# Half slots of an attention stage: all projection steps first, then one block of plain fp32 matmuls and transposes

## The chip, the cores and the metric

The kernel runs on one core of one Trainium2 chip. The metric is the device time of one execution in microseconds (us). The kernel before took 2443.29 us, the median of three runs between 2438.51 and 2446.40 us.

## The reference

The reference is a decoder trunk of two layers over x of 1 x 1024 x 1024 in float32. All of it is causal.

```python
for layer in range(2):
    h = rmsnorm(x, norm_mix[layer])
    x = x + (even_mixer if layer == 0 else swa_mixer)(h, ...)
    h = rmsnorm(x, norm_mlp[layer])
    x = x + square(relu(h @ w_up[layer])) @ w_down[layer]      # hidden width 4096
```

- `even_mixer` projects h by one matrix. Four retention heads (query and key of 64, value and gate of 128) get a rotation, chunks of 128 tokens with a decay matrix and a state that is carried from chunk to chunk, a group norm and a silu gate. Eight heads of width 64 get RMSNorm and rotation of query and key, and attention over a mixture of three dilated windows, (128, 1), (512, 4) and (2048, 16). The two outputs are concatenated and multiplied by `w_out`.
- `swa_mixer` projects to 16 query heads and 4 key and value heads of width 64, with a bias, RMSNorm and rotation; each query sees the last 128 keys; a learned sink adds to the softmax denominator; then an output projection.

## The kernel before

The 1024 tokens are T = 8 tiles of 128 rows. x stays on chip in `X`. The normed input of a stage lies transposed in `hT_hi` and `hT_lo`, and weights lie in `W_hi` and `W_lo`: each fp32 operand is split in two fp32r parts, and one product is three matmuls (`three`, L457 to L461: hi by hi, hi by lo, lo by hi). Scores, transposes, probabilities by values and the whole of retention are plain fp32 matmuls or transposes through `ident`, with no split.

**Two attention stages.** The first (`dr_slots`) holds the dilated heads, two at a time, and the retention heads, one at a time, in NG = 4 groups. A group is 16 slots of projections (8 token tiles of the dilated columns, then 8 of the retention columns), and its other work follows a slot or more behind, so `live` gives for a slot one or two pairs (g, t), t being the slot's number in group g. The second (`s_slots`) holds the sliding window heads, 32 slots of projections and 4 more. Each slot does one projection of 128 tokens by 384 columns: `gemm_steps` is a generator of 8 steps, each step being the three matmuls of one 128-row part of the input (L478 to L492). A slot has two halves, j = 0 and j = 1, with four steps each. Between the steps TensorE does:

- `scores` of attention unit n = 2t + j - 4 (L511, into `sc`), `trans` of unit n - 1 (its probabilities transposed, L543, into `tp`) and `values` of unit n - 2 (L551, into `o_ps`). A unit is one tile of queries with one head (dilated: a + 1 blocks of keys for query tile a, so 1 to 8) or two heads (sliding window: 2 blocks of keys at most each).
- `heads_T` (L564) in the second half: the queries and keys of the tile projected in the slot before are transposed into `qt`.
- retention of chunk r = t - 9: `ret_T` (L570, transposes, at the start of the second half), `ret_scores` (L579, end of the second half), `ret_values` of chunk r - 1 (L587, first half).
- `first_T`, `tile_T`, `norm_T`, `mixed_T`: transposes of whole token tiles where a stage joins its neighbour. `mixed_T` (L494) does so by halves in the slots from O1_T = 30 of the second stage, through `qt`.

**Who waits for whom.** There is no planner; the order is written out by hand, each engine has its own copy of the loop, and semaphores join them. The diff touches TensorE's loop only. For one unit: VectorE reads the scores and makes the masked maximum (`maxima`, L1418 or L1423), ScalarE the exponentials (`probs`, L891 or L898), TensorE `trans`, ScalarE copies `tp` (`probs_T`, L883), TensorE `values`, VectorE scales into `X` (`outputs`, L1440 or L1449). `sc`, `tp`, `o_ps` and `qt` are single buffers. So `scores` waits for the maximum of the unit before (`sm_ready`), and `values` for the scaled output of the unit before (`o_evac`). In VectorE's queue `outputs` of unit n - 3 stands first in a half slot, then `sums`, `maxima` of unit n, `prep` (norm and rotation of the tile's queries and keys, L1389 to L1406, behind GpSimd's L1792, and read by `heads_T`), `ret_rope` (L1331 to L1350, read by `ret_T` from L1340 on) and `ret_out` (L1366 to L1373, behind `ret_values`; it ends in the semaphore `r_x`). `ret_state` (L1354, L1361), behind `ret_scores`, stands in the second half. ScalarE ends a first half with the hi parts of new weights (L827) and a second half with the copies of `qt` (`heads_T_copy`, L905, L907), and opens the slot with the copy of the projection out of PSUM (`evac_G`, L855; in the second stage VectorE does it, L1494) and `head_squares` (L871). GpSimd makes the lo parts of the weights (L1735). The first `head_squares` of a later group waits for the last `ret_out` of the group before, since both use `sq`.

The MLP after each attention stage, and the output projections, are the rest of the kernel; the change does not touch them.

Of the kernel before, what the change touches and what calls it, by code (L numbers as in the profile page):

```python
# [29 lines left out]
def hybrid_trunk(nc, x_in, positions, norm_mix, norm_mlp, w_up, w_down, w_in, w_out0, gn_gain, dq_gain, dk_gain,  # L30
# [7 lines left out]
    S, D = x_in.shape[1], x_in.shape[2]  # L38
    T = S // P
# [49 lines left out]
    with ctx:  # L89
# [166 lines left out]
        def unit(n):  # L256

            return n // (2 * T), n % (2 * T) // 2, n % 2
# [195 lines left out]
        def _(pe):  # L454
# [87 lines left out]
            def trans(kind, n, u0):  # L542
                g, a, j = unit(n)  # L543
                pe.wait_ge(p_ready, u0 + n + 1)
                if u0 + n >= 1:
                    pe.wait_ge(pt_ready, u0 + n)
                for c, to, _, _ in blocks(kind, a):
                    last = nc.tensor.transpose(tp[:, to:to + P], Pm[:, j, c:c + P], ident[:, :])  # L548
                last.then_inc(tp_done, 1)

            def values(kind, n, u0):  # L551
                g, a, j = unit(n)
                pe.wait_ge(pt_ready, u0 + n + 1)
                pe.wait_ge(v_ready, (u0 // 2 if kind == "D" else A_S + (u0 - U_S) // 2) + n // 2 + 1)
                if u0 + n >= 1:
                    pe.wait_ge(o_evac, u0 + n)
                bl = blocks(kind, a)
                v0 = HD * j if kind == "D" else 0
                for m, (_, to, c, e) in enumerate(bl):
                    last = mm(o_ps[:, e * HD:(e + 1) * HD], pT[:, j, to:to + P], V[:, c, v0:v0 + HD],  # L560
                              start=(m == 0 or bl[m - 1][3] != e), stop=(m == len(bl) - 1 or bl[m + 1][3] != e))
                last.then_inc(pv_done, 1)
# [7 lines left out]
            def ret_T(r, n):  # L570

                pe.wait_ge(r_qk, n + 1)
                alone(pe)
                q, k, qx = rQK[:, r % 2, 0:HD], rQK[:, r % 2, HD:2 * HD], QK[:, r % 2, 4 * HD:5 * HD]
                for m, src in enumerate((q, k, qx)):
                    last = nc.tensor.transpose(qt[0:HD, m * P:(m + 1) * P], src, ident[:, :])
                last.then_inc(r_qt, 1)
# [20 lines left out]
            def first_T(s, q):  # L598

                for i in range(T):  # L600
                    if FIRST_T[i] == (s, q):
                        if i in FIRST_DVE:
                            pe.wait_ge(first_dve, FIRST_DVE.index(i) + 1)
                        else:
                            pe.wait_ge(first_pool, FIRST_POOL.index(i) + 1)
                        tile_T(first_xn[i % 6], i, 0, 0)
# [3 lines left out]
            def dr_slots():  # L610

                for s in range(DR_SLOTS):
                    now = live(s)
                    g, t = now[-1]
                    if s < NG * 2 * T:
                        steps = gemm_steps(N_DR + s, t // T, t % T, W, P_DR + 8 * g + 4 * (t // T), 0)
                    else:
                        steps = gemm_steps(N_O0 + s - NG * 2 * T, 0, s - NG * 2 * T, W, P_O0, T)
                    for j in range(2):
                        for g, t in now:  # L620
                            r = t - T - 1
                            if j == 1 and 0 <= r < T:
                                ret_T(r, g * T + r)
                        if s < 2 and j == 0:
                            first_T(s, 0)
                        next(steps)
                        next(steps)
                        if s < 2:
                            first_T(s, 2 * j + 1)
                        for g, t in now:  # L630
                            n, r = 2 * t + j - 4, t - T - 1
                            if 0 <= n < 2 * T:
                                scores("D", n, g * 2 * T)
                            if 0 <= n - 1 < 2 * T:
                                trans("D", n - 1, g * 2 * T)
                            if j == 0 and 0 <= r - 1 < T:
                                ret_values(r - 1, g * T + r - 1)
                        next(steps)
                        for g, t in now:
                            n = 2 * t + j - 4  # L640
                            if 0 <= n - 2 < 2 * T:
                                values("D", n - 2, g * 2 * T)
                        next(steps)
                        if s < 2:
                            first_T(s, 2 * j + 2)
                        for g, t in now:
                            r = t - T - 1
                            if j == 1 and 0 <= r < T:
                                ret_scores(r, g * T + r, g)
                            if j == 1 and 0 <= t - 1 < T:  # L650
                                heads_T("D", t - 1, g * T)
                        if j == 1 and s >= O0_T:

                            pe.wait_ge(r_x, (NG - 1) * T + s - O0_T + 1)
                            tile_T(X[:, s - O0_T, :], s - O0_T, T, 2)

            def s_slots():

                units = NG * 2 * T
                for t in range(S_SLOTS):  # L660
                    c = t // T
                    if t < NG * T:
                        steps = gemm_steps(N_S + t, c % 2, t % T, W, P_S + 4 * c, 3 * T)
                    else:
                        steps = gemm_steps(N_O1 + t - NG * T, 0, t - NG * T, W, P_O1, 4 * T)
                    for j in range(2):
                        n = 2 * t + j - 4
                        next(steps)
                        next(steps)
                        if t == 0:  # L670

                            norm_T(2, T - 2 + j, 3 * T, 1)
                        if 0 <= n < units:
                            scores("S", n, U_S)
                        if t >= O1_T:
                            mixed_T(t - O1_T, 4 * T, j)
                        if 0 <= n - 1 < units:
                            trans("S", n - 1, U_S)
                        next(steps)
                        if 0 <= n - 2 < units:  # L680
                            values("S", n - 2, U_S)
                        next(steps)
                        if j == 1 and 0 <= t - 1 < units // 2:
                            if t >= O1_T:
                                pe.wait_ge(ht_ready, 4 * T + t - O1_T + 1)
                            heads_T("S", t - 1, A_S)
# [1327 lines left out]
```

## Time and profile before

| | |
|---|---|
| runs | 2446.40, 2438.51, 2443.29 us |
| profiled execution | 2441.46 us, of which the span from the first to the last instruction is 2439.7 us |
| PE busy | 2365.9 us (97%), 12184 matmul records |
| PE weight loads busy | 1991.1 us (82%) |
| VectorE, ScalarE, GpSimd busy | 1464.0 (60%), 834.6 (34%), 1099.8 us (45%) |
| chain that ended last, by engine | PE 82%, DVE 10%, POOL 3%, issue 2%, ACT 2%, DMA 1% |
| granted TensorE clock, mean | 0.994 |

A busy share says how long records of an engine were open. For PE the records overlap: the next matmul starts while the last is still draining, so the distance from start to start tells what a matmul costs, and the length of a record does not. A plain fp32 matmul shows as two records. The bracket at the end of a timeline row gives how long that engine was idle just before and which instruction ended the idleness.

### The profile page before, as it was taken

The numbers are of one execution on the slowest core, as the hardware profiler recorded it, in microseconds if no ns is written. First come the engines' busy times: TensorE is split into PE (matmuls) and PEld (weight loads), VectorE is DVE, ScalarE is ACT, GpSimd is POOL, SyncE is SP. The second block draws the span as 40 slices with busy tenths as digits, with TensorE's granted clock in tenths as the row PEclk, the third lists the DMA queues.
The fourth block names the chain that finished last, engine by engine and source line by source line (L and its number), as shares of the span: only waits on it lengthen the run. The fifth ranks groups of instructions, "written<-read, shape, count | busy, mean of one in ns | idle before, by whom it ended". The sixth has DMA issues, their size and how long they took to land.

```text
span 2439.7 us, 34453 instructions
## 1 busy us (share of the span) xinstructions
PE 2365.9 (97%) x12184; PEld 1991.1 (82%) x12184; DVE 1464.0 (60%) x2846; ACT 834.6 (34%) x1717; POOL 1099.8 (45%) x994
## 2 busy tenths in 40 slices
PE   6999999999999999999999899999999999999999
PEld 5777878777987888888888788888977888888887
DVE  7464645546148757675774566663356676667573
ACT  5424333342132322332232455553232232223230
POOL 5123131311227646664673733431245574557461
PEclk9999999999999999999999999999999999999999
DMA  4001010102221021102101300012021102110201
GB/s 136 14 27 27 27 27 14 33 7 87 65 70 52 18 69 60 60 17 69 60 26 57 114 26 24 27 35 91 27 69 61 61 17 69 60 60 17 83 29 78
DMA packets 140981, 120.35 MB, mean 49 GB/s; under 512 B 26048, under 2 KB 126912, under 8 KB 140864
## 3 DMA queue, kind: packets, MB, share of 16 engines
q1 hardware_dynamic: 133488, 103.70, 13.7%
q10 hardware_dynamic: 7376, 15.12, 1.8%
q8 instruction: 70, 1.15, 0.2%
q14 instruction: 47, 0.39, 0.1%
HBM read 110.41 MB, written 8.39 MB: 49 GB/s over the span
## 4 chain that ended last, share of the span: by engine, by line
PE 82%; DVE 10%; POOL 3%; issue 2%; ACT 2%; DMA 1%; SPq 0%; DVEq 0%; ACTq 0%; POOLq 0%
PE gp L459 12%; PE gp L461 12%; PE gp L460 12%; PE sc L459 6%; PE sc L461 6%; PE sc L460 6%; PE o_ps L560 4%; PE sc L526 3%; PE tp L461 2%; PE tp L460 2%; PE tp L459 2%; PE tp L548 2%; PE sc L531 1%; PE qt L461 1%; PE qt L459 1%
## 5 line engine op out<-in xcount | busy, mean ns | idle before, releaser
L459 PE MATMUL gp<-W_hi,hT_hi 128*128 128x384 f32 (+1 forms) x1152 | 423.1, 367 | 6.0 <-DVE hT_lo L1307 6.0
L461 PE MATMUL gp<-W_hi,hT_lo 128*128 128x384 f32 (+1 forms) x1152 | 384.7, 334 | 0.0
L460 PE MATMUL gp<-W_lo,hT_hi 128*128 128x384 f32 (+1 forms) x1152 | 384.0, 333 | 0.0
L1860 POOL TENSOR_TENSOR W_lo<-af,W_hi 128x512 fp32r<-128x512 f32 x168 | 237.5, 1413 | 283.2 <-ACT W_hi L1041 283.2
L1840 POOL TENSOR_TENSOR W_lo<-raw,W_hi 128x1024 fp32r<-128x1024 f32 x72 | 187.2, 2604 | 237.9 <-ACT W_hi L983 225.1
L1554 DVE TENSOR_TENSOR af<-af 128x512 f32<-128x512 f32 x112 | 81.0, 725 | 297.8 <-ACT af L1024 297.7
L1860 POOL TENSOR_TENSOR W_lo<-rb,W_hi 128x512 fp32r<-128x512 f32 x168 | 243.6, 1450 | 0.0
L459 PEld LDWEIGHTS gp<-W_hi,hT_hi 128*128 128x128 f32 x1152 | 221.3, 192 | 15.0 <-issue 6.8
L460 PEld LDWEIGHTS gp<-W_lo,hT_hi 128*128 128x128 f32 x1152 | 221.8, 192 | 0.0
L461 PEld LDWEIGHTS gp<-W_hi,hT_lo 128*128 128x128 f32 x1152 | 219.8, 191 | 0.0
L459 PE MATMUL sc<-hT_hi,W_hi 128*128 128x512 f32 x512 | 200.1, 391 | 5.3 <-DVE hT_lo L1307 5.3
L461 PE MATMUL sc<-hT_hi,W_lo 128*128 128x512 f32 x512 | 199.9, 390 | 0.0
L460 PE MATMUL sc<-hT_lo,W_hi 128*128 128x512 f32 x512 | 199.7, 390 | 0.0
L459 PE MATMUL gp<-hT_hi,W_hi 128*128 128x512 f32 x512 | 199.5, 390 | 0.2 <-POOL W_lo L1840 0.2
L461 PE MATMUL gp<-hT_hi,W_lo 128*128 128x512 f32 x512 | 199.2, 389 | 0.0
L460 PE MATMUL gp<-hT_lo,W_hi 128*128 128x512 f32 x512 | 199.2, 389 | 0.0
L1735 POOL TENSOR_TENSOR W_lo<-raw,W_hi 128x768 fp32r<-128x768 f32 (+1 forms) x70 | 124.4, 1779 | 136.1 <-ACT W_hi L827 135.8
L1041 ACT ACTIVATE W_hi<-af 128x512 fp32r<-128x512 f32 x168 | 105.8, 630 | 165.2 <-PE sc L461 89.4
L883 ACT ACTIVATE pT<-tp 128x512 f32<-128x512 f32 (+7 forms) x128 | 78.3, 612 | 244.9 <-PE tp L548 244.9
L1024 ACT ACTIVATE af<-gp 128x512 f32<-128x512 f32 x56 | 33.4, 601 | 340.3 <-PE gp L461 340.3
L560 PEld LDWEIGHTS o_ps<-V,pT 128*128 128x128 f32 x1056 | 134.8, 191 | 16.1 <-ACT pT L883 8.0
L560 PE MATMUL o_ps<-V,pT 128*128 128x64 f32 x1056 | 133.3, 270 | 10.9 <-DVE X L1440 8.8
(292 smaller groups left out, 5262.7 us busy)
## 6 DMA issues: line engine op xcount, KB each, us to landing
raw<-in_mlp_w_up SPq DMA_DIRECT2D x64, 512.0 KB, 4.2
rb<-in_mlp_w_down SPq DMA_DIRECT2D x56, 512.0 KB, 5.0
raw<-in_hyb_w_in SPq DMA_DIRECT2D x74, 128.0 KB, 2.4
X<-in_x SPq DMA_DIRECT2D x8, 512.0 KB, 7.4
X<-in_x ACTq DMA_DIRECT2D x8, 512.0 KB, 3.4
raw<-in_mlp_w_down SPq DMA_DIRECT2D x8, 512.0 KB, 3.3
raw<-in_swa_w_qkv SPq DMA_DIRECT2D x16, 256.0 KB, 3.2
x_spill<-X ACTq DMA_DIRECT2D x8, 512.0 KB, 2.7
```

The source lines that it names most:

```text
L459: mm(o, a[0], b[0], start=first, stop=False)
L460: mm(o, a[0], b[1], start=False, stop=False)
L461: return mm(o, a[1], b[0], start=False, stop=last)
L526: last = mm(sc[:, c:e], qT[r, a % 2, 0:P], kT[r, c:e], start=True, stop=True)
L548: last = nc.tensor.transpose(tp[:, to:to + P], Pm[:, j, c:c + P], ident[:, :])
L560: last = mm(o_ps[:, e * HD:(e + 1) * HD], pT[:, j, to:to + P], V[:, c, v0:v0 + HD], start=(m == 0 or bl[m - 1][3] != e), stop=(m == len(bl ...
L883: A(pT[:, n % 2, 0:w], tp[:, 0:w], ACT.Copy).then_inc(pt_ready, 1)
L1041: A(WF_hi[:, op_at(side, 2 * p + k)], x(k), ACT.Copy).then_inc(op_hi, 1)
L1554: E.tensor_tensor(x, x, x, ALU.mult).then_inc(a_sq, 1)
L1735: E.tensor_tensor(W_lo[:, slot, c], raw[:, p % 2, 0:n], W_hi[:, slot, c].bitcast(f32), ALU.subtract).then_inc(w_ready, 1)
L1840: E.tensor_tensor(WF_lo[:, at], raw[:, j % 2, :], WF_hi[:, at].bitcast(f32), ALU.subtract).then_inc(w_ready, 1)
L1860: E.tensor_tensor(WF_lo[:, c], x(k), WF_hi[:, c].bitcast(f32), ALU.subtract).then_inc(op_ready, 1)
```

## The change

In `dr_slots` of TensorE a half slot did, before: `ret_T` (second half), two steps, `scores`, `trans` and `ret_values`, one step, `values`, one step, then `ret_scores` and `heads_T`. Now it does four steps, then `scores`, `trans`, `values`, `ret_values`, then `ret_T` at the end of the first half or `ret_scores` and `heads_T` at the end of the second. The transposes of the first slots (`first_T`) keep their place. In `s_slots` the third and fourth step move ahead of `scores`, `mixed_T`, `trans` and `values`. No instruction is added or removed, and no other engine's order changes.

```diff
                     for j in range(2):
-                        for g, t in now:
-                            r = t - T - 1
-                            if j == 1 and 0 <= r < T:
-                                ret_T(r, g * T + r)
                         if s < 2 and j == 0:
                             first_T(s, 0)
                         next(steps)
                         next(steps)
                         if s < 2:
                             first_T(s, 2 * j + 1)
+                        next(steps)
+                        next(steps)
+                        if s < 2:
+                            first_T(s, 2 * j + 2)
                         for g, t in now:
                             n, r = 2 * t + j - 4, t - T - 1
                             if 0 <= n < 2 * T:
                                 scores("D", n, g * 2 * T)
                             if 0 <= n - 1 < 2 * T:
                                 trans("D", n - 1, g * 2 * T)
+                            if 0 <= n - 2 < 2 * T:
+                                values("D", n - 2, g * 2 * T)
                             if j == 0 and 0 <= r - 1 < T:
                                 ret_values(r - 1, g * T + r - 1)
-                        next(steps)
-                        for g, t in now:
-                            n = 2 * t + j - 4
-                            if 0 <= n - 2 < 2 * T:
-                                values("D", n - 2, g * 2 * T)
-                        next(steps)
-                        if s < 2:
-                            first_T(s, 2 * j + 2)
                         for g, t in now:
                             r = t - T - 1
+                            if j == 0 and 0 <= r < T:
+                                ret_T(r, g * T + r)
                             if j == 1 and 0 <= r < T:
                                 ret_scores(r, g * T + r, g)
```

```diff
                             norm_T(2, T - 2 + j, 3 * T, 1)
+                        next(steps)
+                        next(steps)
                         if 0 <= n < units:
                             scores("S", n, U_S)
                         if t >= O1_T:
                             mixed_T(t - O1_T, 4 * T, j)
                         if 0 <= n - 1 < units:
                             trans("S", n - 1, U_S)
-                        next(steps)
                         if 0 <= n - 2 < units:
                             values("S", n - 2, U_S)
-                        next(steps)
```

## Rows read from the trace of the kernel before

**Rows 1.** Windows: length, then busy us (count) by engine, clock, DMA share, GB/s.

```profile
41.00:600.00 559.00, 533.89 (x3014) 437.38 (x3015) 306.77 (x968) 208.83 (x466) 149.71 (x219) 0.99 0.10 29
1384.00:1690.00 306.00, 294.84 (x1955) 254.24 (x1956) 197.39 (x847) 157.40 (x508) 104.66 (x141) 0.99 0.12 34
```

**Rows 2.** Groups of instructions, projection matmuls: busy us, mean ns, idle before.

```profile
L459 PE MATMUL gp<-W_hi,hT_hi 128*128 128x384 f32 (+1 forms) x1152 | 423.1, 367 | 6.0 <-DVE hT_lo L1307 6.0
L461 PE MATMUL gp<-W_hi,hT_lo 128*128 128x384 f32 (+1 forms) x1152 | 384.7, 334 | 0.0
```

**Rows 3.** Timeline of PE, sliding window, one second half: start us, duration us.

```profile
1520.04 0.70 PE L531 MATMUL sc<-kT,qT 64*128 64x256 f32 x4
1520.67 0.66 PE L548 MATMUL tp<-ident,Pm 128*128 128x128 f32 x4
...
1521.52 0.34 PE L461 MATMUL gp<-W_hi,hT_lo 128*128 128x384 f32 x1
1521.69 1.00 PE L560 MATMUL o_ps<-V,pT 128*128 128x64 f32 x8
...
1522.76 0.34 PE L460 MATMUL gp<-W_lo,hT_hi 128*128 128x384 f32 x1
1522.94 0.33 PE L461 MATMUL gp<-W_hi,hT_lo 128*128 128x384 f32 x1
1523.11 0.49 PE L567 MATMUL qt<-ident,QK 128*128 128x128 f32 x3
...
1523.61 0.34 PE L460 MATMUL gp<-W_lo,hT_hi 128*128 128x384 f32 x1
```

**Rows 4.** Waits of PE in 41 to 600 us: us, times, longest.

```profile
PE qt L567 <- DVE QK L1401: 10.3, 4, 3.1
PE o_ps L560 <- DVE X L1440: 8.8, 12, 1.1
PE sc L592 <- DVE rsT L1354: 1.8, 6, 0.3
```

**Rows 5.** Waits of PE in 1380 to 1700 us.

```profile
PE qt L567 <- DVE hT_lo L1293: 5.4, 3, 1.9
...
PE sc L531 <- ACT kT L907: 0.8, 2, 0.6
```

**Rows 6.** Timeline where the second group of the first stage begins.

```profile
172.80 0.38 PE L592 MATMUL sc<-G,rsT 128*128 128x128 f32 x2
...
173.64 0.30 DVE L1366 BATCH_NORM_STATS2 st<-sc 128x6 f32<-128x128 f32 x1 [1.35 <-PE sc L595]
...
180.07 0.69 PE L567 MATMUL qt<-ident,QK 128*128 128x128 f32 x2 [3.15 <-DVE QK L1401]
```

**Rows 7.** Timeline, group 1, slot t = 10 (first chunk of retention meets the last unit).

```profile
263.54 0.39 PE L592 MATMUL sc<-G,rsT 128*128 128x128 f32 x2
...
265.30 0.29 DVE L1366 BATCH_NORM_STATS2 st<-sc 128x6 f32<-128x128 f32 x1
...
269.49 0.29 PE L560 MATMUL o_ps<-V,pT 128*128 128x64 f32 x1 [0.79 <-DVE X L1440]
```

**Rows 8.** Timeline, group 1, slot t = 9: scores, the rotation's end, `ret_T`.

```profile
248.38 0.69 PE L526 MATMUL sc<-kT,qT 64*128 64x512 f32 x1
...
252.77 0.25 DVE L1340 TENSOR_SCALAR QK<-rQK,st 128x64 f32<-128x64 f32 x1
...
253.71 0.38 PE L576 MATMUL qt<-ident,rQK 128*64 128x128 f32 x2
```

**Rows 9.** Timeline, group 1, slots t = 2 and 3: copies of `qt`, `values` of unit 1.

```profile
188.82 0.28 ACT L905 ACTIVATE qT<-qt 128x128 f32<-128x128 f32 x1 [0.57 <-PE qt L567]
...
195.53 0.41 PE L560 MATMUL o_ps<-V,pT 128*128 128x64 f32 x2 [0.94 <-DVE X L1440]
```

**Rows 10.** Timeline of DVE in the half slot of rows 3.

```profile
1520.05 0.29 DVE L1449 TENSOR_TENSOR X<-o_ps,st 128x128 f32<-128x128 f32 x1
```

**Rows 11.** Windows, the stretch around the third group's start.

```profile
319.00:329.00 10.00, 8.34 (x38) 7.52 (x39) 4.68 (x15) 3.98 (x13) 4.10 (x5) 0.83 0.08 21
```

## The prediction

> **What bounds the kernel now.** I read the page first: PE is busy for 97% of the span and makes up 82% of the chain that ended last, so TensorE's own work sets the time, and a wait of PE is paid in full. Then the windows of the two stages that the change touches: PE is busy 534 of 559 us in the first and 295 of 306 us in the second [rows 1]. About 25 and 11 us are idle; that is all that any better order could win from waits. The list of waits says which instruction ends the idleness; most of it is VectorE, at five or six kinds of places [rows 4, 5]. Last I read the timeline around each kind of place, to see from which event the chain that PE waits for starts. The change removes nothing, so two questions are left: does a boundary between fp32r steps and plain fp32 work cost PE anything, and how many microseconds of projection lie, before and after, between the start of a chain and the instruction that waits for its end.
>
> **Boundaries.** The number of separate plain blocks falls: `values` joins `trans` (64 units in each stage, 128 blocks), `heads_T` joins `values` (64), `ret_T` joins `ret_values` (32), so about 224 blocks vanish. What is one worth? The page tempts: L459, the first matmul of each step, shows 367 ns where L461 shows 334 [rows 2], because an L459 behind plain work is drawn longer. But starts decide. Between two projection matmuls lie 0.174 us (1522.76 to 1522.94 rounds it to 0.18). From L461 at 1521.52 over eight records of `values` to L460 at 1522.76 are 1.24 us; take off two projection intervals of 0.174 and 0.89 is left, 0.112 per record. The block of three transposes, 1522.94 to 1523.61, leaves 0.67 - 0.35 = 0.32, or 0.108 each [rows 3]. A fixed price per block would make the block of eight cheaper per record than the block of three; it is not. The boundary costs 0 to 0.02 us. A joint from a transpose straight to a values record is nowhere in the trace. From below: a record hidden behind its neighbour saves 0.08 us, times 128 is 10 us. From above: it costs one record of the kind that the scores show, 0.63 us for four [rows 3], so 0.16, times 128 is 20 us. I take 0, since the records on both sides run at the same 0.11, and keep both ends.
>
> The Trainium skill speaks against long plain blocks: "TensorE: Matmul & The Clock Gate", Part 4: PE-mode transpose, says that transposes do not count as work for the clock. No window of rows 1 shows a mean clock under 0.99; what it would do here is the fourth case below.
>
> **Waits, place by place.** One step is three matmuls at 0.174, so 0.52 us. I count steps from the event that starts a chain to the PE instruction at its end.
>
> 1. *Start of groups 1, 2 and 3.* `ret_values` of the last chunk (172.80) starts the chain over `ret_out`, `head_squares`, `sums`, GpSimd and `prep` to `heads_T` at 180.07, 7.27 us, in which PE stood idle 3.15 us. VectorE had waited 1.35 us for `ret_values` [rows 6], so the chain really starts there. `ret_values` moves from behind two steps to behind four, `heads_T` stays at the end of the slot. The chain starts 1.04 us later: 3 x 1.04 = +3.1 us. Queued behind the waiting `heads_T` are only the next slot's steps, which nobody else needs early.
> 2. *Slot t = 10, four groups.* `values` of unit 15 waits 0.79 us for `outputs` of unit 14, which stands in VectorE's queue behind `ret_out` of chunk 0, and that behind `ret_values` (263.54). VectorE was late on its own and began `ret_out` at 265.30, 1.76 us after `ret_values` began [rows 7]. Now `ret_values` comes two steps (1.04) later, and behind `values` of unit 14, 16 records of 0.112, 1.8 us, which it used to precede: 2.8 us later, with the chain starting 0.4 us after its beginning, so 2.8 - 1.76 + 0.4 = 1.5 us later than now. PE gets to `values` of unit 15 one step later than before in the slot, 0.5. So +1.0 per group, +4.0 us.
> 3. *Slot t = 9, four groups.* `ret_T` of chunk 0 needs `ret_rope`, which VectorE does after the maximum of unit 14. From scores 14 (248.38) the rotation's end (253.02) takes 4.64 us, and `ret_T` starts 5.33 us after the scores [rows 8]. Two steps of the 5.33 move ahead of the scores: 4.29 us are left, 0.35 short, 0.45 with the semaphore. +1.8 us.
> 4. *Slots 30 to 32 of the second stage.* `heads_T` waits for the lo half of `mixed_T` (L1293), 5.4 us in three waits [rows 5]. The chain starts with the scores of the first half slot (maximum, exponentials, copy, lo half, `prep`, `outputs`, and the same in the second half), and two steps move out from between: 3 x 1.04 = +3.1 us.
> 5. *Slots t = 3 and 4 of each group.* Eight of the twelve waits for L1440 are `values` of units 1 and 3, 0.94 us at 195.53. The chain starts at `heads_T` of the slot before, whose copies ScalarE waited 0.57 us for [rows 9]. `heads_T` now comes two steps sooner after the scores, so ScalarE copies as soon as it has its exponentials, about 0.55 us sooner; `values` loses one step, 0.52. Unit 1: 0. Unit 3 comes a slot later in full, gains 0.4 and had 0.24 to wait (0.70 in the first group): -1.0 us in all, between -1.4 and 0.
> 6. *Retention slots.* `ret_values` waits 1.8 us in all for L1354 [rows 4]. It gets two steps more of cover. `ret_T` keeps its distance and becomes the next limit, some 0.4 us further on in each group: -1.5 us, at best -1.8, at worst 0.
> 7. *Second stage, scores behind the copy of `kT`*: 0.8 us [rows 5], two steps more cover, -0.8 us. Elsewhere in this stage the scaled output is done at 1520.34 and `values` comes at 1521.69, 1.35 us in hand; `prep` stands ahead of that output in the queue, so `heads_T` at 1523.11 has over 3 [rows 3, 10]. They lose 0.5 and 1.0: nothing, unless ScalarE, which now meets `heads_T` before it has done the exponentials, runs late; it has about 0.3 us.
> 8. *Clock.* Around one group start the granted clock is 0.83 over 10 us [rows 11]: after the idle stretch the lower level, 1.2 of 2.4 GHz, held for a third of the window, worth up to 1.7 us. Of the six waits in points 1 and 4 four were followed by such a stretch. With a microsecond more each, I count the other one or two in as well: +1.5 us, 0 to +3.
>
> SP's queue and the weight loads follow the steps, whose order against each other and against the slots does not change; DMA keeps 10 to 12% busy [rows 1]. So no transfer moves by more than 2 us, under a slot of lead.
>
> **Sum.** 3.1 + 4.0 + 1.8 + 3.1 - 1.0 - 1.5 - 0.8 + 1.5 = +10.2 us. Against the profiled execution, 2441.5 (span 2439.7 and 1.8 around it), that is 2451.7; this execution lies 1.8 us under the median of the three runs, so the median should come to 2453.5. I say 2453. The positive terms could each fail by a half (-6) or be doubled by their neighbours (+6).
>
> **Rivals.**
> - *The boundary does cost.* A plain block ends with a first projection matmul drawn 0.09 us longer (0.42 against 0.33), and 33 ns times 1152 of L459 are 38 us in the stages with 416 such blocks [rows 2]. If that were time on PE, 224 blocks fewer would win 20 us, less the 10 lost in waits: 2433, faster. It decides if the count of blocks times 0.09 is real; the start-to-start sums speak against it, unless a joined block streams faster than 0.108 a record. 12%.
> - *The waits do not grow.* Every chain starts from an event that moves with the waiting instruction, as in point 5; points 2 to 4 then vanish and point 1 alone stays, with points 6 and 7 against it: +1 to +4, 2446. For it: four places of point 5 work so. Against: VectorE's own waits say where a chain begins in points 1 and 3. 25%.
> - *Joints are dear.* 0.16 us at each of 128 joints adds 20 us: 2474. For it: scores followed by transposes take longer than their records. Against: there the operand's height changes from 64 to 128 rows, here it stays 128. 5%.
> - *Clock.* The longest joined blocks, units 10 to 15 in four groups, are over 3.5 us without a projection matmul. If such a block drops the clock to the lower level as the idle stretches do, at 1.2 to 1.7 us each, 24 blocks add 29 to 41 us: about 2488. The blocks before were up to 2.8 us and no clock fell after one. 4%. The page of the Trainium skill named above would have it so.
>
> **Numbers.** The forecast has 54%, its own range 2445 to 2464. About 0.3%, 7.3 us, is what a measurement of this kernel tells from no change. Faster takes nearly all of the first rival: 0.11. Within 0.3% takes the second and the low third of the forecast's range: 0.30. Slower has the rest: 0.59. The range that leaves out the boundary rival's and the clock's centre and little more is 2440 to 2469.
>
> **What would show it.** PE's records keep their counts; L459's mean falls from 367 towards 350 ns while the distance of starts per step stays 0.52 us. In the waits, L567 behind L1401 grows from 10.3 to 13.4 us, behind L1293 from 5.4 to 8.5, L560 behind L1440 from 8.8 to about 12, with unit 15 at 1.8; L592 and L531 vanish; L576 waits 0.4 us in slot t = 9. If PE's idle time in the two windows grows by 10 us and the time does not, the boundary is worth something. If idle time does not grow, the chains began elsewhere than I say. A transpose followed by a values record at more than 0.12 us shows the dear joint; a clock under 0.99 over the first stage shows the fourth rival.

## The result, and the profile after

The changed kernel takes 2453.15 us, median of seven runs (2450.02 to 2458.45), against 2443.78 us (2438.51 to 2446.40) for the kernel before in the same sessions: ratio 1.0039, 95% interval 1.0029 to 1.0048. That is 0.4% slower and clear of the noise. The forecast was 2453. The profiled execution has a span of 2451.8 us against 2439.7, 12.1 us more, with a mean granted clock of 0.986 against 0.994.

Lines of the changed file are four lower than before (L1436 is `outputs`, L1397 and L1402 end `prep`, L1336 ends the rotation, L1289 is the lo half). The windows of the two stages and the projection groups, to be laid beside [rows 1, 2]:

```profile
41.00:600.00 559.00, 527.49 (x2943) 441.24 (x2944) 285.76 (x944) 202.77 (x463) 148.83 (x216) 0.96 0.10 28
1384.00:1690.00 306.00, 293.92 (x1941) 254.99 (x1939) 190.33 (x840) 155.09 (x508) 112.80 (x152) 0.98 0.11 32
```

```profile
L459 PE MATMUL gp<-W_hi,hT_hi 128*128 128x384 f32 (+1 forms) x1152 | 407.4, 354 | 5.6 <-POOL W_lo L1731 5.0
L461 PE MATMUL gp<-W_hi,hT_lo 128*128 128x384 f32 (+1 forms) x1152 | 388.0, 337 | 0.0
```

In the same 559 us PE gets through 2943 records where it did 3014, and the clock is 0.96 where it was 0.99. The waits of PE in the first stage (first fence) and in the second, beside [rows 4, 5]:

```profile
PE qt L567 <- DVE QK L1397: 13.8, 4, 4.2
PE o_ps L560 <- DVE X L1436: 9.5, 7, 1.8
PE qt L576 <- DVE QK L1336: 8.0, 12, 1.0
```

```profile
PE qt L567 <- DVE hT_lo L1289: 7.1, 3, 2.5
...
PE sc L531 <- ACT kT L903: 1.4, 4, 0.9
PE o_ps L560 <- DVE X L1445: 1.2, 3, 0.4
```

The waits that were forecast are there: `heads_T` at the group starts has gone from 3.1 to 4.2 us, the longest wait of `values` from 1.1 to 1.8 us, L592 no longer waits. The timeline of slot t = 10 in group 1, VectorE and PE, beside [rows 7]:

```profile
265.83 1.90 PE L560 MATMUL o_ps<-V,pT 128*128 128x64 f32 x16
...
267.56 0.44 PE L592 MATMUL sc<-G,rsT 128*128 128x128 f32 x2
267.84 0.38 PE L576 MATMUL qt<-ident,rQK 128*64 128x128 f32 x2
268.04 0.30 DVE L1362 BATCH_NORM_STATS2 st<-sc 128x6 f32<-128x128 f32 x1 [1.41 <-PE sc L592]
...
271.77 0.28 DVE L1436 TENSOR_SCALAR X<-o_ps,st 128x64 f32<-128x64 f32 x1
272.20 0.52 PE L560 MATMUL o_ps<-V,pT 128*128 128x64 f32 x3 [1.79 <-DVE X L1436]
```

`ret_values` of chunk 0 (L592) now stands behind the 16 records of `values` 14. VectorE, which used to come to it late, waits 1.41 us for it, and 4.2 us later PE waits 1.79 us for what VectorE makes at the end of that chain.

Behind that wait something stands that was not in the forecast. Windows over the wait and what follows it (length, then busy us and count by engine, granted clock, DMA share, GB/s):

```profile
270.00:272.00 2.00, 0.41 (x3) 0.09 (x1) 1.93 (x4) 1.47 (x3) 1.52 (x1) 1.00 0.00 0
272.00:273.00 1.00, 0.80 (x6) 0.83 (x6) 0.06 (x1) 0.15 (x1) 0.00 (x0) 0.81 0.24 68
273.00:279.00 6.00, 6.00 (x23) 5.33 (x23) 2.05 (x11) 0.00 (x0) 0.00 (x0) 0.50 0.19 54
```

The granted clock falls within half a microsecond of the end of the wait and stays down for 6.8 us. The first records that it slows are the plain ones of `values` 15, whose starts go from 0.11 to 0.21 us apart. Timeline of PE 5 us further on:

```profile
277.23 0.52 PE L460 MATMUL gp<-W_lo,hT_hi 128*128 128x384 f32 x1
277.55 0.52 PE L461 MATMUL gp<-W_hi,hT_lo 128*128 128x384 f32 x1
277.87 0.52 PE L459 MATMUL gp<-W_hi,hT_hi 128*128 128x384 f32 x1
```

Projection matmuls start 0.32 us apart, where 0.174 is the rule, so the clock is at the lower of its two levels, 1.2 of 2.4 GHz. No such stretch followed `values` 15 in any group of the kernel before.

To weigh these things I cut the first stage at `heads_T` of slot t = 1 of each group. The first three groups, from 38.3 us on, take 421.9 us before and 430.7 after. Of them PE is idle 19.4 and 25.5 us, and projection matmuls with starts over 0.3 us apart lose 3.7 and 6.1 us against 0.174. The rest, 398.8 and 399.0, looks unchanged, but it holds the plain records, which the lower clock slows too. Groups with no slowed projection matmul at all occur in several traces: 132.4 and 132.6 us each without idle time in the order of before (kernel `s_apart` below), 130.6 and 130.7 in the order of after (`ret_first`, where only two neighbours inside a block are swapped, and `d_only`). So at full clock a group is 1.85 us shorter after, and the low clock costs three groups about 5 us before (3.7 and 1.3 in plain records) and 13 after (6.1 and 7.0). The granted clock itself says much the same: in these groups PE worked at the lower level for 12.6 us before and 30.8 after, and at 0.146 us lost in every 0.32 that is 6 and 14 us.

### The profile page after: what moved, and what is told of

Read it like the earlier page. It is cut to its first block, busy times and chain, and to the rows that moved or that the text cites. A ratio compares the mean times of both kernels' runs of the same rounds, so it can differ in the third digit from the quotient of the medians.

```text
span 2451.8 us, 34453 instructions
## 1 busy us (share of the span) xinstructions
PE 2372.2 (97%) x12184; PEld 2009.4 (82%) x12184; DVE 1442.0 (59%) x2846; ACT 827.3 (34%) x1717; POOL 1102.0 (45%) x994
## 4 chain that ended last, share of the span: by engine, by line
PE 86%; DVE 7%; POOL 2%; issue 2%; ACT 2%; DMA 1%; SPq 0%; DVEq 0%; ACTq 0%; POOLq 0%
PE gp L459 13%; PE gp L461 13%; PE gp L460 13%; PE sc L459 6%; PE sc L460 6%; PE sc L461 6%; PE o_ps L560 4%; PE sc L526 3%; PE tp L548 3%; PE tp L460 2%; PE tp L459 2%; PE tp L461 2%; PE sc L531 2%; PE qt L459 1%; PE o_ps L459 1%
## 5 line engine op out<-in xcount | busy, mean ns | idle before, releaser
L459 PE MATMUL gp<-W_hi,hT_hi 128*128 128x384 f32 (+1 forms) x1152 | 407.4, 354 | 5.6 <-POOL W_lo L1731 5.0
L461 PE MATMUL gp<-W_hi,hT_lo 128*128 128x384 f32 (+1 forms) x1152 | 388.0, 337 | 0.0
L460 PE MATMUL gp<-W_lo,hT_hi 128*128 128x384 f32 (+1 forms) x1152 | 387.4, 336 | 0.0
L459 PEld LDWEIGHTS gp<-W_hi,hT_hi 128*128 128x128 f32 x1152 | 223.2, 194 | 12.7 <-issue 7.8
L460 PEld LDWEIGHTS gp<-W_lo,hT_hi 128*128 128x128 f32 x1152 | 223.6, 194 | 0.0
L461 PEld LDWEIGHTS gp<-W_hi,hT_lo 128*128 128x128 f32 x1152 | 222.6, 193 | 0.0
L459 PE MATMUL sc<-hT_hi,W_hi 128*128 128x512 f32 x512 | 200.1, 391 | 5.3 <-DVE hT_lo L1303 5.3
L460 PE MATMUL sc<-hT_lo,W_hi 128*128 128x512 f32 x512 | 199.9, 390 | 0.0
L461 PE MATMUL sc<-hT_hi,W_lo 128*128 128x512 f32 x512 | 199.8, 390 | 0.0
L459 PE MATMUL gp<-hT_hi,W_hi 128*128 128x512 f32 x512 | 199.4, 389 | 0.0
L461 PE MATMUL gp<-hT_hi,W_lo 128*128 128x512 f32 x512 | 199.2, 389 | 0.0
L460 PE MATMUL gp<-hT_lo,W_hi 128*128 128x512 f32 x512 | 199.2, 389 | 0.0
```

The lines of the kernel that those rows point to most:

```text
L459: mm(o, a[0], b[0], start=first, stop=False)
L460: mm(o, a[0], b[1], start=False, stop=False)
L461: return mm(o, a[1], b[0], start=False, stop=last)
```

## Experiments

The theory at the start, A: the time moves by how many projection steps lie between the start of a chain and the PE instruction at its end; boundaries are free. B: each boundary between fp32r and plain work costs 0.09 us. C: the long joined blocks themselves lower the clock.

**The two stages apart.** `s_only` has the new `s_slots` and the old `dr_slots`, `d_only` the other way round; the lines are those of the change.

```diff
 # s_only: s_slots as changed, dr_slots as before
 # d_only: dr_slots as changed, s_slots as before
```

> The changed order in the sliding window stage alone. Theory A (what moves the time is how many projection steps lie between the start of a chain and the PE instruction that waits for it; a block boundary costs nothing): the trace of the full change had in this stage 0.3 us more idle time, 1.9 us more of slowed projection matmuls and 8 slots shorter by 0.5 us when idle time is taken out, so +0.5 to +2 us on 2443.8, no difference that can be told. Rival B (a boundary between fp32r and plain fp32 costs 0.09 us): 96 boundaries fewer in 32 slots, -8.6 us plus the same 2: about 2437. Rival C (long plain blocks by themselves lower the clock): blocks of 2.1 us with every half slot, so +5 us and more with a clock under 1.00 in the steady slots.

> The changed order in the dilated and retention stage alone. Theory A: +10 to +12 us, nearly all of the full change (2454 to 2456), with the same waits as there: heads_T 4.19 us at three group starts, values of unit 15 1.8 us at four places, ret_T 0.38 us at four. Rival B: 128 boundaries fewer here, -11 us beside waits of +6.5 and slowed matmuls of +5.7: about 2445. Rival C: as A in the sum, but the slowed matmuls follow the longest blocks (units 10 to 15), not the idle stretches.

Measured beside 2441.67 us for the kernel before: `s_only` 2446.31 us, ratio 1.0015 (1.0005 to 1.0024), and `d_only` 2454.09 us, 1.0041 (1.0027 to 1.0054). Nearly all of the loss is the first stage's. The interval of `s_only` leaves out 1, but its trace does not put that time into the second stage: the stage takes 294.5 us before and 295.7 in `s_only`, within the 0.5 to 2 us expected, and the rest of the 5.9 us between the spans stands ahead of it, where the code is the same, PE's idle time grew by 0.4 us and the clock was lower. In the second stage eight steady slots are 68.0 us without idle time instead of 68.5, with the clock at 1.00 all through, so C is not seen there and B is far too large; slots 30 to 32 give the gain back. In `d_only` the waits are those of the full change. The slowed matmuls stood behind the idle stretches, not behind the longest blocks, in three groups of four; in the first group there were none.

**`ret_values` alone goes back.** All attention blocks stay joined.

```diff
                             first_T(s, 2 * j + 1)
+                        for g, t in now:
+                            r = t - T - 1
+                            if j == 0 and 0 <= r - 1 < T:
+                                ret_values(r - 1, g * T + r - 1)
                         next(steps)
...
-                            if j == 0 and 0 <= r - 1 < T:
-                                ret_values(r - 1, g * T + r - 1)
```

> The full change, but ret_values goes back behind the second step of the first half slot, as before the change. Every attention block stays joined. Theory A: the wait at the three group starts falls from 4.19 to 3.15 us (-3.1), that of values 15 from 1.8 to about 0.3 (-6), the slowed matmuls behind values 15 go (-5), the joint of ret_values and ret_T is lost (+1.6) and ret_values may wait 0.3 us again in a few slots: 2440 to 2443. Rival C (the joined blocks lower the clock): slowed matmuls stay, 2445 to 2448. If the loss had to do with scores, values and heads_T standing together: no change, 2453.

2434.58 us, ratio to before 0.9960 (0.9945 to 0.9975), 18.6 us under the changed kernel. The same change with this one instruction group left in its place is faster than the kernel before. (That is against the changed kernel's own session; each beside the kernel before in its session, it is 19.3 us.) Waits of PE in its first stage, and the window:

```profile
PE qt L567 <- DVE QK L1399: 12.3, 6, 3.2
PE qt L576 <- DVE QK L1338: 5.1, 9, 0.8
PE o_ps L560 <- DVE X L1438: 2.7, 5, 1.0
```

```profile
41.00:620.00 579.00, 552.99 (x3162) 460.93 (x3162) 302.17 (x981) 211.36 (x473) 158.38 (x226) 0.99 0.12 34
```

Against the changed kernel the three groups are 17.9 us shorter: 7.5 of idle time, 13 of clock, and 2.6 back for `ret_values` standing alone again. I had expected 10 to 13; the waits came as said, and the clock is what I had too small.

**Which part of the placement.** `ret_first` keeps the four steps and puts `ret_values` ahead of `values`; `ret_last` moves only the last chunk of a group back behind two steps. Both edits are against the changed kernel.

```diff
 # ret_first
+                            if j == 0 and 0 <= r - 1 < T:
+                                ret_values(r - 1, g * T + r - 1)
                             if 0 <= n - 2 < 2 * T:
                                 values("D", n - 2, g * 2 * T)
-                            if j == 0 and 0 <= r - 1 < T:
-                                ret_values(r - 1, g * T + r - 1)
 # ret_last
+                        for g, t in now:
+                            if j == 0 and t == 2 * T + 1:
+                                ret_values(T - 1, g * T + T - 1)
                         next(steps)
...
-                            if j == 0 and 0 <= r - 1 < T:
+                            if j == 0 and 0 <= r - 1 < T - 1:
```

> The full change, but ret_values stands ahead of values in the block; it still comes after four steps. Theory A: VectorE begins ret_out of chunk 0 by its own lateness again, so the wait at values 15 falls from 1.8 to about 0.3 us in four places (-6), and with it the slowed matmuls behind that wait; the group starts keep 4.19 us. Of the 18.6 us between the full change and ret_values behind two steps this placement should win 10 to 12: about 2442. If the two steps alone matter and not the 1.8 us of values ahead: 2450 or more.

> The full change, but ret_values of the last chunk of each group alone (slot t = 17) goes back behind the second step. Theory A: the three waits at the group starts fall from 4.19 to 3.15 us (-3.1) and some of the slowed matmuls behind them go (0 to -4); the waits at values 15 stay 1.8 us. 2446 to 2450. With ret_first it should add up to the 18.6 us of both. If the clock falls for the long plain blocks, it changes nothing in the slowed matmuls.

`ret_first` 2442.61 us, ratio 0.9990 (0.9981 to 1.0000), `ret_last` 2449.02 us, 1.0021 (1.0011 to 1.0031), beside 2445.41. From 2453.15 they win 10.5 and 4.1 us, both within what was expected. Together 14.6 of 18.6, or 16.4 of 19.3 when each is taken by its ratio to the kernel before in its session; those sessions differ by 2 to 4 us in the kernel before, so the sum is not tested closer. The profile of `ret_last` is of its fastest run, 2440.63 us. Waits of `ret_first` (first fence) and of `ret_last`, first stage:

```profile
PE qt L567 <- DVE QK L1397: 13.8, 4, 4.2
PE qt L576 <- DVE QK L1336: 10.0, 15, 1.0
PE o_ps L560 <- DVE X L1436: 3.6, 6, 0.9
```

```profile
PE qt L567 <- DVE QK L1400: 10.7, 4, 3.2
PE o_ps L560 <- DVE X L1439: 9.5, 7, 1.8
```

Each touches one kind of wait and leaves the other.

**The one move alone.** The order of before, and only `ret_values` goes behind the fourth step. No attention block is joined.

```diff
-                            if j == 0 and 0 <= r - 1 < T:
-                                ret_values(r - 1, g * T + r - 1)
...
                         for g, t in now:
                             r = t - T - 1
+                            if j == 0 and 0 <= r - 1 < T:
+                                ret_values(r - 1, g * T + r - 1)
                             if j == 1 and 0 <= r < T:
                                 ret_scores(r, g * T + r, g)
```

> The order of before, with ret_values alone moved to behind the fourth step, where it joins ret_T. No attention block is joined. Theory A, as it now stands (waits, the clock after them, and 0.1 us for each ret_values that joins ret_T): the three waits at group starts grow to 4.2 us (+3.1), that of values 15 from 0.8 to 2.3 us (+6), the clock falls behind it in most groups (+4 to +8), 28 joints win 3: +10 to +14 us, 2454 to 2458 on 2443.8, so this one move is enough for the whole loss. Rival D (the loss needs the joined blocks too, since they lower the clock): the waits as said, but no slowed matmuls behind values 15: +5 to +6.

2465.99 us, ratio 1.0085 (1.0071 to 1.0099) beside 2445.66: +20.3 us, more than the full change and well over the 10 to 14 that I expected. The waits are as computed, the clock is not. Its waits and its window:

```profile
PE o_ps L560 <- DVE X L1440: 14.4, 12, 2.3
PE qt L567 <- DVE QK L1401: 12.8, 4, 4.2
```

```profile
41.00:620.00 579.00, 542.57 (x2999) 450.45 (x2999) 307.17 (x964) 210.17 (x469) 150.29 (x218) 0.96 0.10 28
```

This settles C. With no joined attention block, but 2.3 us of waiting at `values` 15, the low clock follows in three groups of four; in `ret_first`, with the same long block and 0.4 us of waiting (0.65 in the last group), in one. Over all twelve traces, four groups each: behind a wait of 1.8 us or more at that place, 12 of 16; behind 0.3 to 1.1 us, 1 of 32. It is the idle stretch, with or without the joined blocks.

**Boundaries doubled.** In the second stage `scores` moves ahead by a step, so that each part stands alone.

```diff
                         next(steps)
+                        if t < O1_T and 0 <= n < units:
+                            scores("S", n, U_S)
                         next(steps)
...
-                        if 0 <= n < units:
+                        if t >= O1_T and 0 <= n < units:
                             scores("S", n, U_S)
```

> The order of before; in the second stage up to slot 29 scores moves ahead by one step, so scores, transposes, values and heads_T each stand alone: two boundaries more per slot, some 60 in all. Theory A (a boundary costs 0 to 0.02 us): 0 to +1 for them, and the three waits of 0.70 us for the output fall to 0.2: 2441 to 2444, no difference that can be told; 8 slots of the steady part take 68.5 us without idle time, as before. Rival B (0.09 us each): +5.4, and 8 slots take 70 us without idle time.

2452.41 us, ratio 1.0038 (1.0026 to 1.0051) beside 2445.41. A is wrong here and B is nearer: eight steady slots take 69.8 us without idle time instead of 68.5, 1.3 us for 16 more boundaries, 0.08 each (B said 0.09). The rest is waiting: `scores` has a step less of cover behind the copy of `kT` and now waits 0.12 us in every first half. Timeline of PE in one half slot:

```profile
1505.15 0.34 PE L461 MATMUL gp<-W_hi,hT_lo 128*128 128x384 f32 x1
1505.42 0.70 PE L531 MATMUL sc<-kT,qT 64*128 64x256 f32 x4
1506.05 0.44 PE L459 MATMUL gp<-W_hi,hT_hi 128*128 128x384 f32 x1
1506.33 0.34 PE L460 MATMUL gp<-W_lo,hT_hi 128*128 128x384 f32 x1
1506.50 0.34 PE L461 MATMUL gp<-W_hi,hT_lo 128*128 128x384 f32 x1
1506.68 0.60 PE L548 MATMUL tp<-ident,Pm 128*128 128x128 f32 x4
1507.03 0.42 PE L459 MATMUL gp<-W_hi,hT_hi 128*128 128x384 f32 x1
1507.29 0.34 PE L460 MATMUL gp<-W_lo,hT_hi 128*128 128x384 f32 x1
1507.47 0.34 PE L461 MATMUL gp<-W_hi,hT_lo 128*128 128x384 f32 x1
1507.64 1.00 PE L560 MATMUL o_ps<-V,pT 128*128 128x64 f32 x8
...
1508.71 0.34 PE L460 MATMUL gp<-W_lo,hT_hi 128*128 128x384 f32 x1
```

The scores alone cost 1.18 - 0.35 = 0.83 us from L461 to L460, the values still 1.24 - 0.35 = 0.89 as in [rows 3]. The transposes alone cost 0.79 - 0.35 = 0.44 us, 0.11 each, which leaves nothing for a boundary. In this half slot the two come to 1.27 us where together they were 1.22. What the split adds stands with the scores: the boundary that costs is the one behind a 64-row operand.

**`values` behind the fourth step.** The order of before, with one step more of cover for `values`, in both stages. The diff shows the first; the second has the same move.

```diff
-                        for g, t in now:
-                            n = 2 * t + j - 4
-                            if 0 <= n - 2 < 2 * T:
-                                values("D", n - 2, g * 2 * T)
                         next(steps)
+                        for g, t in now:
+                            n = 2 * t + j - 4
+                            if 0 <= n - 2 < 2 * T:
+                                values("D", n - 2, g * 2 * T)
```

> The order of before, with one move in both stages: values goes from behind the third step to behind the fourth, so it joins heads_T, and everything else stays. Theory A: each wait of values falls by one step of 0.52 us: unit 1 of four groups 0.94 to 0.42, unit 3 to nothing (-1.4 in all), unit 15 0.8 to 0.3 (-2), and three of 0.7 to 0.2 in the second stage (-1.5): -5.5 to -7.5 us, about 2437. Rival B: 64 boundaries fewer besides, another -6: 2431. If what waits for values (the outputs, and behind them the maximum) then comes late, the gain is lost again: 2443.

2432.53 us beside 2441.67, ratio 0.9958 (0.9945 to 0.9971), 9.1 us. Waits of `values` fall from 10.9 to 4.0 us in all, 6.9 us and within the 5.5 to 7.5 that A gave to the waits. The time won is more, because the joints win something too: eight steady slots of the second stage are 0.32 us shorter for eight joints of `values` with `heads_T`, 0.04 each.

**A faster version.** Put together from the above: `values` behind the fourth step in the first stage, the last chunk's `ret_values` behind the first, the joined block in the second stage up to slot 29, and `values` behind the fourth step from slot 30 on.

```diff
 # first stage, beside the move of v_late
                         next(steps)
+                        for g, t in now:
+                            if j == 0 and t == 2 * T + 1:
+                                ret_values(T - 1, g * T + T - 1)
                         next(steps)
...
-                            if j == 0 and 0 <= r - 1 < T:
+                            if j == 0 and 0 <= r - 1 < T - 1:
                                 ret_values(r - 1, g * T + r - 1)
 # second stage
+                        if t < O1_T:
+                            next(steps)
+                            next(steps)
                         if 0 <= n < units:
                             scores("S", n, U_S)
...
-                        next(steps)
+                        if t >= O1_T:
+                            next(steps)
+                            next(steps)
                         if 0 <= n - 2 < units:
                             values("S", n - 2, U_S)
-                        next(steps)
```

> What the runs so far point to, put together: in the first stage the order of before with values behind the fourth step, and ret_values of a group's last chunk already behind the first step; in the second stage the joined block up to slot 29 and values behind the fourth step from slot 30 on. Theory A against values behind the fourth step alone (2432.5): three waits of 3.15 us fall by one step (-1.6), the steady part of the second stage is 0.35 us per 8 slots shorter (-1.4): 2429 to 2431. Rival: at the group start GpSimd or ScalarE is what ends last, and the one step is lost: 2431 to 2433.

2429.12 us beside 2445.41, ratio 0.9942 (0.9925 to 0.9958). The waits at the group starts are 2.63 us, one step less than 3.15. In its first stage:

```profile
PE qt L567 <- DVE QK L1408: 8.1, 4, 2.6
PE o_ps L560 <- DVE X L1447: 3.7, 9, 0.6
```

And with `ret_values` of chunks 1 to 6 joined to `ret_T`:

```diff
-                            if j == 0 and 0 <= r - 1 < T - 1:
+                            if j == 0 and r - 1 == 0:
                                 ret_values(r - 1, g * T + r - 1)
...
+                            if j == 0 and 1 <= r - 1 < T - 1:
+                                ret_values(r - 1, g * T + r - 1)
```

> The fastest so far (2429.1), and ret_values of chunks 1 to 6 behind the fourth step, where it joins ret_T; that of chunk 0 stays behind the second step, that of the last chunk behind the first. Theory A: VectorE begins ret_out of these chunks some 2 us after ret_values in slots 11 to 13, so nothing waits longer; 24 joints at 0.1 us win 2.4, and ret_values no longer waits 0.3 us for rsT while ret_T may: 2425 to 2428. Rival: the joints are worth nothing, as the prediction had it: 2429.

2428.01 us beside 2445.66, ratio 0.9934 (0.9919 to 0.9949), the fastest of the study, but not to be told from `best`: the three groups are 4.0 us shorter without idle time and slowed matmuls counted out (part of that is clock), and wait 4.6 us more, at `ret_T` (0.6 us in two slots of a group) and `heads_T`. The joint is worth at least what was said; that nothing waits longer was wrong.

## Why the prediction was right, and where it was not

The direction, the places and the four large waits were right. The total was right because two terms that I had wrong cancel: the clock and the boundaries. That 2453 met the median to 0.2 us is luck. PE's idle time over the whole trace grew by 5.7 us (70.1 to 75.8), where the forecast's waits add up to 8.7. Term by term, from the two traces:

| term | forecast | measured |
|---|---|---|
| 1 group starts | +3.1 | +3.1 (3 x 4.18 to 4.19 against 3 x 3.15) |
| 2 `values` 15 | +4.0 | +3.7 (7.2 against 3.5) |
| 3 `ret_T`, slot t = 9 | +1.8 | +1.5 (4 x 0.38, none before) |
| 4 slots 30 to 32 | +3.1 | +2.9 (`heads_T` 7.1 against 5.4, and 1.2 at `values`) |
| 5 slots t = 2 to 4 | -1.0 | -2.6 |
| 6 retention slots | -1.5 | +0.8 |
| 7 second stage, other | -0.8 | -2.5 |
| 8 clock | +1.5 | about +17 |
| boundaries | 0 | about -9.5 |

The measured column comes to +14.4 us. PE's idle time outside these places, most of it ahead of 43 us, fell by 1.1 us, which leaves 13.3 where the spans differ by 12.1. So the two large terms, clock and boundaries, are known to a microsecond or two and not better.

- Points 1 to 4 stand. The method, to find the event from which a chain really starts and to count steps from there, gave the waits of points 1 to 3 to 0.1 us. In point 4 it gave the sum and not the place: `heads_T` grew by 1.7 us and not 3.1, and 1.2 us stand at `values`, which the point does not name. `retv_two`, `ret_first` and `ret_last` took those of points 1 and 2 away one by one.
- Point 5: the sign is right. Unit 1 gained more than "0": its wait is gone in two groups of four, though a new one of 1.3 us stands at `heads_T` of the first.
- Point 6 failed on its "next limit". `ret_T` already waited in the kernel before, which [rows 4] leave out (us, times, longest, first stage):

```profile
PE qt L576 <- DVE QK L1340: 3.6, 5, 0.8
```

Now it is 8.0 us in 12, of which 1.5 belong to point 3. It waits 0.52 us in slot 14 of three groups and about 1 us in each of the last five slots, where 0.7 stood before. In the last five slots the lo part of a token tile (L1303, 1.23 us) stands ahead of the rotation in VectorE's queue, which I had not followed.
- Point 7: the copy of `kT` did not gain, because ScalarE now comes to it late, as the point feared. The three waits of 0.7 us at `values` vanished, since the chain moved ahead a little and missed GpSimd's split: the copy L1406 ahead of `outputs` took up to 1.7 us beside it, and now 0.20 us at most.
- Point 8 was mis-sized by a factor of ten. I asked which of the old low-clock stretches would grow and missed that the grown wait at `values` 15 would make new ones, in all four groups of that trace, each 6.8 us long with the plain records in it. The granted clock stood at the lower level for 28 us in the trace before and for 70 after, 27 of the 41 us more behind `values` 15, 10 at the group starts and 3 in slots 30 to 32. Of the two, PE was idle in 1 and 5 us; the rest at 0.146 us lost in every 0.32 gives +17. One pair of traces overstates it somewhat: the mean clock of all seven runs is 0.987, that of the 25 runs of the kernel before in a later session 0.993, and among those 25 each 0.001 of clock goes with 2.1 us, so about 14 us.
- The boundary: "costs 0 to 0.02 us" came from two kinds of block and was laid on all 224. It holds for `values` behind `trans` (0.2 us for 16 in eight steady slots of the second stage, 0.01 each) and for nothing else: `values` with `heads_T` 0.04, `ret_values` with `ret_T` 0.11 (0.85 us in a group of eight, 131.5 against 130.65). In all 4 x 1.85 for the first stage and 4 x 0.53 for the second, 9.5 us (these prices explain the second stage's share; of the first stage's 1.85 they explain about 1.4). My first rival had a true core, at half its price. The joint from a transpose to a values record, for which I took 0, costs nothing. Timeline of PE, changed kernel, to be laid beside [rows 3]:

```profile
1500.26 0.70 PE L531 MATMUL sc<-kT,qT 64*128 64x256 f32 x4
1500.89 0.65 PE L548 MATMUL tp<-ident,Pm 128*128 128x128 f32 x4
1501.38 1.00 PE L560 MATMUL o_ps<-V,pT 128*128 128x64 f32 x8
1502.19 0.42 PE L459 MATMUL gp<-W_hi,hT_hi 128*128 128x384 f32 x1
1502.45 0.34 PE L460 MATMUL gp<-W_lo,hT_hi 128*128 128x384 f32 x1
```

From the scores to L460 are 2.19 us; apart they were 1.30 (1520.04 to 1521.34) and 1.24 for the values with two projection intervals of 0.35, 2.19 as well.

- The rivals "the waits do not grow" and "joints are dear" are refuted by the rows above. The fourth, that the long blocks would lower the clock, named the right quantity and the wrong cause. The rule of the Trainium skill that I had set beside it ("TensorE: Matmul & The Clock Gate", Part 4) is not borne out by these runs as a ground for it: blocks of up to 5.2 us of transposes and plain matmuls kept the full clock in `retv_two`, where the long wait was missing. Of such a block eight transposes make up only 0.9 us, so the rule on transposes by themselves is not tested here.

What stays open: why about one in four of the long waits is followed by no slow stretch, and how the 4 us between 14.6 and 18.6 divide; with one profile for each kernel and sessions that differ by 2 to 4 us neither can be told. The clock also varies where nothing was changed: in the first three groups of `s_only`, whose code is that of the kernel before, PE worked at the lower level for 9.8 us against 12.6. And it is shown that the long wait brings the clock down, not what decides it in the one case of four.

## What to carry to other kernels

When a block of work is moved, list for each instruction in it who waits for it on another engine, and move the head of the longest such chain last or not at all: here one group of instructions, `ret_values`, turned a gain of 7 to 10 us into a loss of 9. A wait that grows toward 2 us on TensorE was here worth its length and more than as much again for the clock behind it, and should be priced so until a trace says otherwise. A boundary between operand kinds is to be measured for each kind of block, by distances from start to start, before one price is laid on all.

## What the runs showed of the hardware

- A 1.8 to 2.3 us idle stretch of PE within a slot of mostly plain work was followed, 0.2 to 2.7 us after its end, by a stretch at 1.2 GHz in 12 of 16 cases; idle stretches of 0.3 to 1.1 us at the same place in 1 of 32. The low clock more than doubled the cost of the waits: 2.0 us of waits (at the group start and at `values` 15) and 2.8 us of clock in the changed kernel against before (7.8 and 5.1 against 5.8 and 2.3, group 1).
- Leaving a block of plain scores on 64 rows for fp32r matmuls costs about 0.08 us (1.3 us for 16 in `s_apart`), leaving one of values or transposes on 128 rows 0.01 to 0.04 us.
- The lengths of the records mislead: L459's mean fell from 367 to 354 ns although the clock was lower (0.986 against 0.994).
- The time of a run follows its mean granted clock: the 25 runs of the kernel before in one session have clocks of 0.991 to 0.995 and times of 2448.1 to 2439.5 us, and all seven of the changed kernel lie at 0.985 to 0.989.
